# Sixteen transposes of a state space layer's output move into the middle of a projection tile, and two weight copies move behind the gelus

## What is computed

```
proj = xn @ w_in[i]
q, k, v, u, gates = jnp.split(proj, splits, axis=-1)
...
s = s5_layer(u, ...)
...
# inside s5_layer
y = (C_re x_re - C_im x_im + d_skip * u).reshape(bsz, seq, SSM_WIDTH)
g = jax.nn.gelu(y)
out = g * jax.nn.sigmoid(g @ w_glu + b_glu)
```

## Time and profile before

| | |
|---|---|
| time, median of 3 runs | 1398.07 us (1397.95 to 1398.42) |
| time of the profiled execution | 1397.82 us |
| its span | 1396.0 us |
| PE busy | 1374.4 us, 98% of the span |
| ACT busy | 835.6 us, 60% |
| DVE busy | 697.0 us, 50% |
| POOL busy | 204.9 us, 15% |

### The profile page before, as it was taken

How to read it: one execution, slowest core, us unless ns; L and a number is a source line. 1 busy time by engine, 2 the same in 40 slices (tenths; PEclk the granted TensorE clock), 3 DMA queues, 4 the chain that set the end, 5 groups by cost and what they waited for, 6 DMA issues and landing times.

```text
span 1396.0 us, 18365 instructions
## 1 busy us (share of the span) xinstructions
PE 1374.4 (98%) x6660; PEld 1114.1 (80%) x6660; DVE 697.0 (50%) x1328; ACT 835.6 (60%) x1217; POOL 204.9 (15%) x240
## 2 busy tenths in 40 slices
PE   9999899999999999999999999999999999999998
PEld 6888677777788888888888877777798888888887
DVE  7996278988743455554145154745255201213324
ACT  8573777777665656665356366765667654535443
POOL 1120110100111111111111111100111111111112
PEclk9999999999999999999999999999999999999999
DMA  9997776676579888788978887755678798887873
GB/s 280 239 190 158 199 178 156 140 167 146 123 201 229 187 189 194 190 204 185 212 179 188 191 190 183 157 141 118 150 167 195 175 213 187 196 199 179 207 167 91
DMA packets 86246, 252.67 MB, mean 181 GB/s; under 512 B 16784, under 2 KB 24080, under 8 KB 86160
## 3 DMA queue, kind: packets, MB, share of 16 engines
q0 software_dynamic: 32400, 116.93, 46.0%
q1 hardware_dynamic: 51776, 130.90, 30.9%
q10 hardware_dynamic: 1984, 3.70, 0.8%
HBM read 126.98 MB, written 3.41 MB: 93 GB/s over the span
## 4 chain that ended last, share of the span: by engine, by line
PE 89%; DVE 4%; DMA 3%; ACT 2%; issue 1%; SPq 0%; DVEq 0%; ACTq 0%
PE pg L656 25%; PE pg L658 25%; PE pg L657 25%; DMA w_lo<-w_raw 2%; PE py L948 1%; PE ps L868 1%; PE ps L845 1%; PE ps L846 1%; PE ps L847 1%; PE ps L1133 1%; PE ps L1141 1%; DMA w_raw<-weights 1%; DMA act_lo<-w_raw 1%; PE py L1151 1%; DVE rstd L1887 0%
## 5 line engine op out<-in xcount | busy, mean ns | idle before, releaser
L656 PE MATMUL pg<-x_hi,w_hi 128*128 128x512 f32 x992 | 391.3, 394 | 2.2 <-DVE gates L1887 1.6
L658 PE MATMUL pg<-x_hi,w_lo 128*128 128x512 f32 x992 | 386.4, 389 | 0.0
L657 PE MATMUL pg<-x_lo,w_hi 128*128 128x512 f32 x992 | 386.2, 389 | 0.0
L614 POOL DMA_DIRECT2D w_lo<-w_raw x221 | 190.8, 863 | 1153.8 <-ACT w_lo L1264 1070.6
L1263 ACT ACTIVATE w_hi<-w_raw 128x1024 fp32r<-128x1024 f32 (+1 forms) x213 | 222.4, 1044 | 129.6 <-PE pg L658 93.5
L656 PEld LDWEIGHTS pg<-x_hi,w_hi 128*128 128x128 f32 x992 | 186.2, 188 | 50.6 <-issue 12.3
L1264 ACT ACTIVATE w_lo<-w_raw 128x1024 fp32r<-128x1024 f32 (+1 forms) x213 | 221.1, 1038 | 0.0
L658 PEld LDWEIGHTS pg<-x_hi,w_lo 128*128 128x128 f32 x992 | 186.2, 188 | 39.2
L657 PEld LDWEIGHTS pg<-x_lo,w_hi 128*128 128x128 f32 x992 | 186.3, 188 | 38.7 <-issue 1.0
L656 PE MATMUL pg<-act_hi,w_hi 128*128 128x512 f32 x424 | 165.1, 389 | 0.1
L657 PE MATMUL pg<-act_lo,w_hi 128*128 128x512 f32 x424 | 165.0, 389 | 0.0
(11 more groups left out here) (467 smaller groups left out, 1980.3 us busy)
## 6 DMA issues: line engine op xcount, KB each, us to landing
w_raw<-weights SPq DMA_DIRECT2D x218, 512.0 KB, 4.8
w_lo<-w_raw POOLq DMA_DIRECT2D x213, 512.0 KB, 5.7
kq_rot<-kq_raw SPq DMA_DIRECT2D x64, 64.0 KB, 2.1
w_raw<-weights SPq DMA_DIRECT2D x8, 384.0 KB, 3.8
w_lo<-w_raw POOLq DMA_DIRECT2D x8, 384.0 KB, 4.3
hid<-x SPq DMA_DIRECT2D x8, 256.0 KB, 5.4
hid<-x ACTq DMA_DIRECT2D x8, 256.0 KB, 5.0
act_lo<-w_raw POOLq DMA_DIRECT2D x4, 512.0 KB, 7.3
```

What stands on the lines that cost most here:

```text
L614: pool.dma_start(low_of(u)[:, 0:n], w_raw[:, s, 0:n], accum_op=ALU.add).then_inc(lo_in[s], 16)
L656: pe.matmul(bank[:], wh, xh(k), start=n == 0, stop=False)
L657: pe.matmul(bank[:], wh, xl(k), start=False, stop=False)
L658: last = pe.matmul(bank[:], wl, xh(k), start=False, stop=n == len(ks) - 1)
```

## The change

The sixteen transposes leave their place behind unit q0 and stand inside it, in front of the matmuls of its fourth k tile. In ACT's program the four gelus stand in front of the two weight copies of v6, where they stood behind them. Nothing is added or removed.

```diff
             chunk_outputs(0)
             chunk_outputs(1)
-            named(("q", 0), XH, XL)
-            output_turns(0)
-            output_turns(1)
+            def turns_inside(k):
+                if k == 3:
+                    output_turns(0)
+                    output_turns(1)
+
+            named(("q", 0), XH, XL, ahead_of=turns_inside)
             pe.wait_ge(blocks_made, 1)
             kq_sums(0, "k", 0)
             values(1)
...
             kq_out(0, "k", 0, "kg")
             act.dma_start(rtab[:], rope).then_inc(r_landed, 16)
-            ahead(("q", 0))
             turned_out(0)
             turned_out(1)
+            ahead(("q", 0))
             ps_read(act, ("yt", 0))
             ps_read(act, ("yt", 1))
```

## The result

The changed kernel takes 1390.92 us (median of 5), the one before 1398.07 us: 7.15 us less, a ratio of 0.995 with an interval of 0.9936 to 0.9965. Two more sets of five runs of the same changed kernel gave 1391.15 against 1398.02 and 1390.13 against 1398.25. The forecast was 7.98 us less, 1390.1. Two single executions further down, of 4896.07 and 2793.73 us, are left out of the medians of their kernels.

The account below looks back on a forecast made before the run. PE, busy 98% of the span, bounds the kernel and loses 6.0 us waiting before v4 plus a slow clock; 6.21 of idle and start and 1.77 of clock make 7.98, so 1398.07 - 7.98 = 1390.1 us, range 1389.0 to 1392.4.

Parts of the forecast that it names:

- The stall is one of ACT's order: In front of v4: PE waits 6.0 us because ACT's gelus queue behind v6's weight copies, whose load lands at 141.40.
- 7.98 us up to the end of v4, 6.21 of wait and 1.77 of clock: PE's gain by v4's end, from 154.06 to 146.08: 6.21 us of idle and start, 1.77 of slow clock.
- No wait inside q0, `ps0` free 2.15 us early: Transposes at 135.03 inside q0 cost no wait; gelus free `ps0` at 138.5, 2.15 us before PE wants it.
- v6's copies at 141.40 as before: On ACT behind the gelus: v6's load lands at 141.40 unchanged, so its copies stand at 141.40 to 143.4.
- the 5.25 us: ACT's work behind v6's copies moves up by 5.25 us, not 8; `g_hi` begins at 143.43 and not 148.68.
- v7's low part is the tightest point, 1.0 us early: v7's low weights, issued at 150.2, land at 156.4; PE wants them at 157.4; before, they were 3.7 us early.
- the rival that had a chance of 0.15: v7's weights come late: a low part of 8.6 us lands 1.4 us late, gain 6.6, time 1391.5; chance 0.15.
- Further on, ACT is paced by PE again: After v7: the copies at 159.76 had waited 1.45 us for a v5 matmul; glu0 moves from 170.84 to 162.9.
- from there each engine waits for PE or for a chain that starts at PE, so the 8 us stay: From glu0 on, every engine follows PE, so the 8 us gained are kept to the end.
- the gain is handed back later: Rival for 140.80:188.00: weights' transfers can't keep up, gain shrinks, to nothing at worst, 1398; chance 0.04.
- The share of 0.94: Transfers' busy share after the change: 36.8 us of work from 140.80:188.00, 0.78 before, in 39.2 us.
- The 3.2 us for a low part: Skill page's estimate for v7's 512 KB low part, landing at 153.4; the prediction used the rows' 6.2 us instead.

## Why the prediction was right

**The stall is one of ACT's order.** Right. The gelus alone ahead of the copies bring nearly everything, the transposes alone bring nothing.

**7.98 us up to the end of v4, 6.21 of wait and 1.77 of clock.** Right: 7.96 us between the two profiles, once the 0.40 us are taken off by which the profiled execution was late when it came to the change. The clock's part by itself was 1.9 us in the times.

**No wait inside q0, `ps0` free 2.15 us early.** No run shows a wait inside q0. Of the slack the runs show that it is at least 1.8 us, the part that moving the transposes back used up without a visible wait.

**v6's copies at 141.40 as before.** Off: they stand at 142.70, 142.29 and 143.49 in the three profiles of the changed kernel. Less the 0.40 to 0.61 us by which these executions came late to q0, the load landed 0.5 to 1.5 us later than in the profile of before. SP had issued it at 138.96 against 137.62 (first profile), since one of its transfers of `kq_raw` took it 1.53 us to issue instead of 0.59. An issue of 0.96 to 1.84 us stands there in all nine profiles that have the transposes inside q0, and in none of the three others; why is open. It cost nothing at v6, but ACT's work behind the copies moved up by as much less than the 5.25 us: v7's low part was issued at 151.38, where 150.2 was worked out, 150.6 with the 0.40 us.

**v7's low part is the tightest point, 1.0 us early.** The place is right, the margin was smaller: it landed 0.2 us before PE wanted it in the first profile (157.63 against 157.84) and 0.6 us in the second, and in the third it cost the 0.3 us. Its own length, 6.3 us in all three, was as the sum had it (6.2). So this was not the rival that had a chance of 0.15, a longer low part, but the late load of v6.

**"Further on, ACT is paced by PE again", and "from there each engine waits for PE or for a chain that starts at PE, so the 8 us stay."** This is the step that failed, and it explains 0.5 to 3.0 us. Before, ACT waited 1.45 us for PE ahead of glu1's copies, and so glu1's low part was issued just behind q1's load:

```profile
161.73 0.33 SPq L524 DMA_DIRECT2D w_raw<-weights  x1
162.06 0.86 POOL L614 DMA_DIRECT2D w_lo<-w_raw  x1 [2.60 <-ACT w_lo L1264]
```

After, PE is so far ahead that these copies, at 154.13, wait for nothing, and the two have changed places:

```profile
156.41 0.86 POOL L614 DMA_DIRECT2D w_lo<-w_raw  x1 [1.03 <-ACT w_lo L1267]
157.65 0.33 SPq L524 DMA_DIRECT2D w_raw<-weights  x1
```

The low part moved up by 5.65 us. The load, which starts when v7's low part has landed, moved up by 4.08. It then took 7.9 to 10.0 us in the three profiles, where the load in this place took 5.8 before. The sum had no term for this load, nor for the two copies, the table load and the sigmoid behind it. That sigmoid had next to no slack even before:

```profile
175.33 0.69 ACT L1494 ACTIVATE hid<-pg,prm 128x512 f32<-128x512 f32 x1
```

It ended at 176.02, and PE began glu's third tile at 176.28. In the profile after, ACT stood idle for 1.88 us of the load's 8.80, so by an estimate a load of 6.9 us would have cost nothing. The prediction's rival "the gain is handed back later" named transfers that don't keep up in just this stretch, and gave it 0.04 as a total loss; it came as a partial one in each of the three profiles. The share of 0.94 that it worked out for the 39.2 us was about right (0.92 measured over 140.80:180.00), but it is a mean. Ten microseconds of it stand at 1.06:

```profile
157.00:167.00 10.00, 10.00 (x46) 8.24 (x45) 0.69 (x1) 5.80 (x9) 1.13 (x2) 1.00 1.06 250
```

The share alone doesn't tell a short load from a long one, though: the kernel before has 0.98 in the same window, and so has the one with glu1's copies put off, and neither has a wait of PE on the sigmoid.

7.98 less a wait of 0.5 to 1.7 gives 6.3 to 7.5 us, and the three sets measured 7.15, 6.87 and 8.12. The last is more than its own profile allows (7.98 - 3.0 - 0.3). But that profile is of the slowest of its five executions, 1393.54 us, and the other four took 1389.99, 1390.12, 1390.13 and 1393.04. The three profiled executions of the changed kernel go in the order of their waits: 1390.64 us with 0.5, 1392.14 with 1.7, 1393.54 with 3.0 and 0.3. So the medians probably stand for executions with a short wait; which wait an unprofiled one had can't be seen. Nothing in the sum kept the wait short, so that the time came out within 1.1 us of 1390.1 in all three sets is in part luck.

**The 3.2 us for a low part.** By the fit on the Trainium skill's page "DMA: Bandwidth & Descriptors" (Anatomy of one DMA — SWDGE (gpsimd) path) v7's low part would have had 4 us to spare. It took 6.3 us in the profile after, and glu1's low part, two behind it, 9.8. The same page's sentence that transfers issued by any engine run on the same 16 DMA engines (Issuing engines are not separate DMA queues) fits what the runs show: SP's load took 4.8 us instead of 8.8 when POOL's transfers were put off.

## What to carry to other kernels

When a wait is taken away, list every chain behind it by how far it moves: here PE moved up by 8 us, ACT was worked out to move by 5.25, and the landing of v7's low part moved by 4.1. Where a slow mover meets the fast one, slack is lost (3.5 us for that low part, from 3.7 to 0.2), and at glu's first sigmoid more was lost than there was. Look too at each wait that goes away: it had held something back, here a transfer that then got in front of another. In a queue that runs in order, put the short instruction that frees a bank ahead of one that waits for a transfer; the old stall and the new one are the same pattern in two places. Look at the transfers' share in windows as short as one unit's chain, since a mean of 0.9 hides a stretch without reserve, and in such a stretch at who is issued first.

## What the runs showed of the hardware

A table load doesn't wait with the instruction behind it. In the run with ACT's part alone it ran at 135.95, and the gelu then waited 3.16 us for PE; so its 1.28 us lay in the shadow of a wait.

The same 512 KB load of q1's weights took 3.9 to 10.2 us in the twelve profiles: 3.9, 4.5, 4.8 and 5.8 us where POOL's low part for glu1 was issued behind it, and 7.8 to 10.2 where it was issued 1.2 to 1.4 us ahead of it.

The granted clock stayed at 1.00 in a 6 us wait for data when matmuls that nobody needs kept PE busy for 5.55 us of it, and the unit behind was 1.75 us shorter for it (5.46 against 7.21).

Open: in the first 30 us PE's longest wait for `raw_lo` is 1.8 to 2.2 us in the three profiles of the changed kernel, and 0.8 in the one of before. The kernel that only adds matmuls shows 1.5 and the one with the transposes alone 2.0, and no edit lies there, so I take it for a difference between executions; it wasn't examined.
